# Twenty places instead of eighteen for the expert matrices of a hybrid decoder step

## What is computed

```python
def grouped_moe(h, w_router, b_router, w_gate, w_up, w_down):
    logits = (t @ w_router) + b_router
    probs = jax.nn.softmax(logits, axis=-1)
    # best group of 4 experts, then the best two experts in it -> comb[token, expert]
    act = jax.nn.silu(jnp.einsum('td,edf->tef', t, w_gate)) * jnp.einsum('td,edf->tef', t, w_up)
    act = act * comb[..., None]
    y = jnp.einsum('tef,efd->td', act, w_down)

def layer(x, c, past, ssm0, conv0, w, w_router, b_router):
    # adaLN; forgetting attention and Mamba-2 branch on h @ w_in; m = their gated sum
    x = x + gt1 * (m @ w['w_o'])
    h2 = rms_norm(x, w['g_norm2']) * (1 + sc2) + sh2
    x = x + gt2 * grouped_moe(h2, w_router, b_router, w['w_gate'], w['w_up'], w['w_down'])
```

## Time and profile before

| | |
|---|---|
| median of three runs | 815.74 us (815.09 to 819.5) |
| the profiled execution | 816.63 us, of it 815.0 us from the first to the last instruction |
| mean granted TensorE clock | 0.973 of full speed |
| TensorE busy | 764.1 us, 94% |
| bytes moved | 219.67 MB, 270 GB/s over the span |

### The profile page before, as it was taken

One profiled execution on the slowest core, in us unless ns is written; L12 is line 12 of the kernel. 1 busy time (PEld: TensorE's weight loads), 2 busy tenths in 40 slices (PEclk: granted clock), 3 DMA queues, 4 the chain that ended last, 5 costly groups with the idle time before them and its releaser, 6 DMA issues.

```text
span 815.0 us, 12510 instructions
## 1 busy us (share of the span) xinstructions
PE 764.1 (94%) x4573; PEld 531.0 (65%) x4573; DVE 366.3 (45%) x847; ACT 294.5 (36%) x731; POOL 95.4 (12%) x156
## 2 busy tenths in 40 slices
PE   3698999999998999999989999999599999999997
PEld 3475687778775777888878788888333444444434
DVE  2455457777772275687998201123211223121213
ACT  1213247656772135658873001013211222221213
POOL 3321011222101115221011000000000000000000
PEclk9999999999999999999999899999599999999999
DMA  9797465879866522369998984373679999999992
GB/s 289 239 355 225 148 179 165 293 238 317 273 228 207 157 62 68 101 182 396 335 293 293 333 314 132 114 281 136 256 301 418 421 420 422 420 420 421 421 418 93
DMA packets 93531, 219.67 MB, mean 270 GB/s; under 512 B 11792, under 2 KB 67672, under 8 KB 78980
## 3 DMA queue, kind: packets, MB, share of 16 engines
q1 hardware_dynamic: 78850, 181.71, 61.4%
q0 software_dynamic: 7984, 31.87, 11.9%
q10 hardware_dynamic: 6634, 5.25, 2.1%
HBM read 207.58 MB, written 13.22 MB: 271 GB/s over the span
## 4 chain that ended last, share of the span: by engine, by line
PE 63%; DMA 10%; SPq 9%; ACT 7%; DVE 5%; issue 3%; POOLq 1%; ACTq 1%; POOL 0%; DVEq 0%
PE bank L1639 14%; PE bank L1949 9%; PE bank L1870 7%; SPq L559 5%; PE bank L1971 5%; DMA out_ssm_sample<-arena 4%; PE bank L1572 4%; PE bank L1878 4%; PE bank L1635 4%; DMA arena<-in_w_down 3%; PE bank L1852 3%; PE bank L1990 2%; SPq L540 2%; PE bank L1593 1%; DVE conv_work L1305 1%
## 5 line engine op out<-in xcount | busy, mean ns | idle before, releaser
L1639 PE MATMUL bank<-h_normed,weight_ring 128*128 128x264 f32 x1024 | 238.9, 390 | 3.0 <-ACT conv_work L1005 3.0
L1639 PEld LDWEIGHTS bank<-h_normed,weight_ring 128*128 128x128 f32 x1024 | 192.9, 191 | 38.3 <-issue 3.5
L1949 PE MATMUL bank<-arena,h_normed 128*64 128x512 f32 x176 | 79.3, 606 | 0.0
L1870 PE MATMUL bank<-y_T,weight_ring 128*128 128x264 f32 x256 | 59.6, 397 | 0.0
L1949 PE MATMUL bank<-weight_ring,h_normed 128*64 128x512 f32 x192 | 56.3, 595 | 0.6 <-ACT h_normed L1047 0.6
L1870 PEld LDWEIGHTS bank<-y_T,weight_ring 128*128 128x128 f32 x256 | 50.1, 196 | 8.9
L1498 DVE TENSOR_TENSOR arena<-arena,bank 128x512 f32<-128x512 f32 x8 | 8.7, 1090 | 104.7 <-PE bank L1949 104.7
L1505 DVE SCALAR_TENSOR_TENSOR x_residual<-bank,modulation,x_residual 128x256 f32<-128x256 f32 x64 | 28.8, 484 | 57.9 <-PE bank L1990 57.9
L1572 PE MATMUL bank<-identity,arena 128*128 128x128 f32 (+5 forms) x236 | 32.0, 277 | 15.3 <-ACT arena L840 9.5
L1572 PEld LDWEIGHTS bank<-identity,arena 128*128 128x128 f32 (+5 forms) x236 | 26.8, 148 | 26.0 <-issue 11.7
L997 ACT ACTIVATE arena<-conv_out,expanded 128x128 f32<-128x128 f32 x128 | 38.3, 388 | 13.0 <-DVE arena L1381 11.1
(11 more groups left out here) (360 smaller groups left out, 1182.7 us busy)
## 6 DMA issues: line engine op xcount, KB each, us to landing
weight_ring<-in_w_in SPq DMA_DIRECT2D x36, 1024.0 KB, 5.8
weight_ring<-in_w_mod SPq DMA_DIRECT2D x22, 1024.0 KB, 9.8
arena<-in_w_up SPq DMA_DIRECT2D x14, 1024.0 KB, 20.0
weight_ring<-in_w_gate SPq DMA_DIRECT2D x14, 1024.0 KB, 20.1
arena<-in_w_down SPq DMA_DIRECT2D x11, 1024.0 KB, 26.8
weight_ring<-in_w_up SPq DMA_DIRECT2D x10, 1024.0 KB, 18.7
arena<-in_state_ssm POOLq DMA_DIRECT2D x8, 1024.0 KB, 8.7
out_ssm_sample<-arena POOLq DMA_DIRECT2D x8, 1024.0 KB, 9.4
```

The costliest lines, as they stand in the source:

```text
L1639: ins = mm(ps[:, 0:T], w, hT[:, c, :], start=c == 0, stop=c == KD - 1)
L1870: ins = mm(ps[:, 0:T], w, yT[:, c, :], start=c == 0, stop=c == NXB - 1)
L1949: ins = mm(banks[i][BLK * e:BLK * e + BLK, :], xg[:, 4 * h + c, BLK * e:BLK * e + BLK], ws[e][:, c, :], start=h == 0 and c == 0, stop=h == ...
```

## The change

Two places are added, so that NMS is 20.

- Place 16 is new: a tensor "early_small" of 128 x 2048 words takes the place of eight small tensors, which become slices of it. att_T and conv_work move to places 17 and 18.
- Place 19 is new and is in two parts of 4 KB a partition: the second half of the h2tok rows in conv_out (uf[:, D:D + 1024]) and 1024 words of a tensor "head_rows", in which head_work, dt_logf and cums now lie side by side. A piece in it is loaded by two DMAs of 512 KB, and its semaphore counts 48 instead of 32 a use, which it shares with place 18.
- SP issues m = 16 right behind m = 15, without waiting for ("hx", 2, 1); m = 17 behind that wait; m = 18 and m = 19 behind h2_st; freed(m - 20) starts with m = 20.
- TensorE takes its operands through rows_of, which finds the part; shapes, order and number of matmuls are as they were.

```diff
-        half += [attT[:].rearrange("p c t -> p (c t)")[:, 0:2048], work[:, 0:2048]]
-        NMS = len(half)
+        half += [early[:, 0:2048], attT[:].rearrange("p c t -> p (c t)")[:, 0:2048], work[:, 0:2048]]
+        quarter = (uf[:, D:D + 1024], heads[:, T:T + 1024])
+        NMS = len(half) + 1
+
+        def rows_of(s, kind, c):
+
+            w = (512, 512, 1024)[kind]
+            if s == NMS - 1:
+                return quarter[c * w // 1024][:, c * w % 1024:c * w % 1024 + w]
+            return half[s][:, c * w:c * w + w]
+
+        def landed_per_use(s):
+
+            return 48 if s // 2 == (NMS - 1) // 2 else 32
...
-                sp.dma_start(half[s], (wg, wu, wdn)[kind][2 * j + e][:, 2048 * h:2048 * h + 2048]).then_inc(moe_full[s // 2], 16)
+                src = (wg, wu, wdn)[kind][2 * j + e][:, 2048 * h:2048 * h + 2048]
+                if s == NMS - 1:
+                    for q in range(2):
+                        sp.dma_start(quarter[q], src[:, 1024 * q:1024 * q + 1024]).then_inc(moe_full[s // 2], 16)
+                else:
+                    sp.dma_start(half[s], src).then_inc(moe_full[s // 2], 16)
...
             load_expert(7)
+            load_half(16)
             filled_by(("hx", 2, 1))
-            load_half(16)
+            load_half(17)
             sp.wait_ge(h2_st, 48)
-            load_half(17)
+            load_half(18)
+            load_half(19)
             for m in range(NMS, 12 * NPAIR):
                 freed(m - NMS)
                 load_half(m)
...
-                        pe.wait_ge(moe_full[s // 2], (r * moe_uses(s) + use) * 32)
-                    ws.append(half[s].rearrange("p (k n) -> p k n", k=(4, 4, 2)[kind]))
+                        pe.wait_ge(moe_full[s // 2], (r * moe_uses(s) + use) * landed_per_use(s))
+                    ws.append([rows_of(s, kind, c) for c in range((4, 4, 2)[kind])])
```

More of the change, by code:

```diff
@@ L66, in build @@
         ident = sb("identity", [128, 128])
-        ntri = sb("neg_triangle", [128, 3 * 128 + 1])
-        triu = sb("upper_triangle", [128, 128])
+        early = sb("early_small", [128, 2048])
+        ntri, triu = early[:, 0:385], early[:, 385:513]
         onesf = sb("ones", [128, 128])
-        blk = sb("head_blocks", [128, 128])
+        blk = early[:, 513:641]
         striu = sb("strict_upper", [128, 128], BF16)
@@ L82, in build @@
         brow = sb("router_bias", [1, NE])
-        cT = sb("cond_T", [128, KD, 32])
-        wfd = sb("w_forget_dt", [128, KD, HB])
+        cT = early[:, 1025:1281].rearrange("p (k n) -> p k n", k=KD)
+        wfd = early[:, 641:1025].rearrange("p (k n) -> p k n", k=KD)
         wr = sb("w_router_sb", [128, KD, NE])
@@ L96, in build @@
         yT = yq[:, 0:NXB * T].rearrange("p (c t) -> p c t", c=NXB)
-        fd = sb("dt_logf", [HB, T])
-        acsT = sb("cums", [64 + HB, NP])
+        heads = sb("head_rows", [128, 4 * T + NP])
+        fd = heads[0:HB, 3 * T:4 * T]
+        acsT = heads[0:64 + HB, 4 * T:4 * T + NP]
         ex = sb("expand_in", [SH, 2 * NS + 1])
-        tokc = sb("token_cols", [128, 7 * 32])
+        tokc = early[:, 1537:1761]
         lft = sb("logf_tok", [128, 3, NH])
-        exo = sb("expanded", [128, NXB * (2 * NS + 1)])
+        exo = early[:, 1761:2033]
         dsk = exo[:, 0:NXB]
@@ L106, in build @@
         sm2 = sb("small", [128, 64])
-        fdw_all = sb("head_work", [128, 3, T])
+        fdw_all = heads[:, 0:3 * T].rearrange("p (a t) -> p a t", a=3)
         fdw = fdw_all[0:HB]
         tokrow = fdw_all[:, 0, :]
-        mrow = sb("mod_rows", [128, SW])
+        mrow = early[:, 1281:1537]
         stT = sb("conv_states", [128, NCB, 24])
@@ L461, in build @@
         o_fs = sem("ssm_prompt_stored")
-        moe_full = [sem(f"expert_half_pair_landed{i}") for i in range(9)]
+        moe_full = [sem(f"expert_half_pair_landed{i}") for i in range(10)]
         gate_half = sem("gate_first_half_used")
@@ L662, in _ @@
                                  pattern=[[-1, 128]], channel_multiplier=1), consts)
-            link(g.memset(cT[:], 0.0), consts)
+            link(g.memset(cT, 0.0), consts)
             link(g.memset(onesf[:], 1.0))
             link(g.memset(epsc[:], EPS))
-            link(g.memset(blk[:], 0.0))
+            link(g.memset(blk, 0.0))
             link(g.memset(blk[0:64, 0:64], 1.0))
@@ L669, in _ @@
             link(g.memset(qbd[:], 0.0), qbd_zero)
-            link(g.memset(ntri[:], -1.0))
-            link(g.affine_select(out=ntri[:], in_=ntri[:], compare_op=ALU.is_ge, fill=0.0, base=-128,
+            link(g.memset(ntri, -1.0))
+            link(g.affine_select(out=ntri, in_=ntri, compare_op=ALU.is_ge, fill=0.0, base=-128,
                                  pattern=[[1, 385]], channel_multiplier=-1))
-            link(g.affine_select(out=triu[:], in_=onesf[:], compare_op=ALU.is_ge, fill=0.0, base=0,
+            link(g.affine_select(out=triu, in_=onesf[:], compare_op=ALU.is_ge, fill=0.0, base=0,
                                  pattern=[[1, 128]], channel_multiplier=-1))
@@ L865, in _ @@
                 if k == "mod":
-                    release(act, fn(mrow[:], ps[:, 0:SW], ACT.Copy), j)
+                    release(act, fn(mrow, ps[:, 0:SW], ACT.Copy), j)
                 elif k == "ssq":
@@ L1337, in _ @@
                     release(dve, v.tensor_tensor(cbm, ps.rearrange("p (g k) -> p g k", g=SG),
-                                                 triu[:].unsqueeze(1).to_broadcast([128, SG, 128]), ALU.mult), j)
+                                                 triu.unsqueeze(1).to_broadcast([128, SG, 128]), ALU.mult), j)
                 elif k == "ab":
@@ L1641, in _ @@
                     pe.wait_ge(qk_sq, 1 if k == "kn" else 2 + j[1] // 4)
-                    ins = mm(ps[:, 0:T], blk[:], u[:, j[1] % 4, :], start=True, stop=True)
+                    ins = mm(ps[:, 0:T], blk, u[:, j[1] % 4, :], start=True, stop=True)
                 elif k == "kt":
@@ L1949, in gate_up @@
                                 ins = mm(banks[i][BLK * e:BLK * e + BLK, :], xg[:, 4 * h + c, BLK * e:BLK * e + BLK],
-                                         ws[e][:, c, :], start=h == 0 and c == 0, stop=h == 1 and c == 3,
+                                         ws[e][c], start=h == 0 and c == 0, stop=h == 1 and c == 3,
                                          tile_position=(0, BLK * e))
@@ L1971, in down @@
                                 ins = mm(banks[2 + q][BLK * e:BLK * e + BLK, :], aT[:, 2 * h + c, BLK * e:BLK * e + BLK],
-                                         ws[e][:, c, 512 * q:512 * q + 512], start=h == 0 and c == 0,
+                                         ws[e][c][:, 512 * q:512 * q + 512], start=h == 0 and c == 0,
                                          stop=h == 1 and c == 1, tile_position=(0, BLK * e))
```

## The result

| | before | after |
|---|---|---|
| median of 20 runs each | 816.89 us (814.43 to 824.24) | 820.6 us (815.77 to 824.99) |
| ratio | | 1.0037, 95% interval 1.002 to 1.0054 |
| profiled execution's span | 815.0 us | 818.9 us |
| mean granted TensorE clock | 0.973 | 0.972 |
| TensorE busy | 764.1 us | 766.4 us |

The kernel became slower by 3.0 us, with an interval of 1.6 to 4.4 us. That is under the 0.5% within which I had called it the same, but 820.6 us lies above my range of 812.9 to 818.9. The kernel before also came out at 816.89 us over 20 runs, where three had given 815.74.

A forecast was written before the change was run, and what follows sets the result against it. TensorE was taken to bound the expert stage. Waits -2.3, store +0.2 and first gather +2.9 summed to +0.8 us: 815.8 on the profiled span of 815.0, 816.5 on the median of 815.74; range 812.9 to 818.9.

The forecast's parts named there:

- What bounds the kernel: Expert stage: TensorE is the bound at 26.8 us a pair; transfers cost it 2.3 us at the very end.
- The rival in which the transfers bind: Expert stage: transfers are the bound, so two pieces less gain 5.0 us, to 810.8; chance 0.05.
- the two waits: TensorE's two waits for weights in the down matrices of pair 6 both go, a gain of 2.3 us.
- The slices and the divided place: Small tensors as slices cost zero; divided-place pieces take 2.64 us instead of 2.49, 0.45 us together, hidden by unused lead.
- the change doesn't do what it says: Late stream: something else sets the landings, the waits stay at 2.3 and the start costs 3.1: 818.8; chance 0.06.
- Piece 16 ahead of the stores: Before the experts: the early piece delays the last 32 KB store by 0.2 us, bounds 0 and 2.5.
- landed together with the end of everything, so the queues share: Last store: its landing with pieces 12 to 15 was read as sharing, the ground for taking 0.2 us.
- First in, first out: Last store: upper bound of 2.5 us if it waits behind every byte issued earlier.
- Pieces 17 to 19 beside the gather: First gather takes 7.7 us instead of 4.8, landing 2.9 us later at about 589.5, when all queued bytes are through.
- The clock: TensorE's slow matmuls at the experts' start shift with it; taken as zero, at most 1.7 us either way.
- The start that costs nothing: Store and gather don't feel the added pieces, only the waits go: 813.4, or 814.4 with 1 us on the gather; chance 0.27.
- transfers in line: Between hx's last row and the first expert matmul: bytes in issue order, store +2.5, gather +5.2, to 821.1; chance 0.12.

The follow-up runs named there:

- layout_only: The kernel before with only the small tensors laid out as slices, 18 places and the old load order: 818.62 us, ratio 1.0014.
- start_as_before: The changed kernel with 16 and 17 at their old points, 18 and 19 only after the gather landed: 815.99 us, ratio 0.9981 to the kernel before.
- after_fourth: The changed kernel run again unaltered: ratio 1.003 to the kernel before.
- after_fifth: The changed kernel run again unaltered, a second time in the same job: ratio 1.0006 to the kernel before.
- the two runs with two pieces behind: The changed kernel with 18 and 19 issued only after the first gather landed, run twice: 815.39 and 813.12 us, ratios 0.9974 and 0.993 to before.
- before_copy: The kernel before, unaltered, timed as if it were an experiment: 817.74 us, ratio 1.0006.
- four_behind_gather: The changed kernel with pieces 16 to 19 issued only after the first gather landed: 813.83 us, ratio 0.9954 to the kernel before.
- kept_busy: four_behind_gather plus six unread matmuls in TensorE's waits before the experts: 811.22 us, ratio 0.9925 to the kernel before.
- none_ahead: The changed kernel with 16 issued together with 17 behind the sample rows of hx, run twice: 818.38 and 818.62 us, ratios 1.0009 and 0.9996 to before.
- before_two_behind_gather: The kernel before, 18 places, with pieces 16 and 17 issued only after the first gather landed: 816.92 us, ratio 0.998.

## Why the prediction was off

**What bounds the kernel: right.** With 20 places TensorE waits for no weights and pairs stay at 26.82 us. The rival in which the transfers bind needed 5.0 us from the stream; it gave 2.6, where I had counted 2.3 for the two waits.

**The slices and the divided place: right.** layout_only shows no cost, and start_as_before, with the divided place in use, has its gain of 2.4 us in full. That the change doesn't do what it says is excluded.

**Piece 16 ahead of the stores: wrong.** I took 0.2 us between bounds of 0 and 2.5. In after_fourth and after_fifth, whose transposes were not slow throughout, the store takes 6.37 and 5.16 us, and 5.64 and 5.74 in the two runs with two pieces behind; the four profiles of the old order (before, before_copy, layout_only, start_as_before) have 4.52 to 4.88. That is 0.3 to 1.9 us, about 1. What the early piece costs beyond the store follows under the next heading.

Counted from A the landing goes 15.3 to 15.45 with neither piece 16 nor 17 issued by then (four_behind_gather, kept_busy), 16.9 to 17.65 in the order of before, 17.66 to 18.42 with 16 up front, and 19.25 to 19.37 in the three with slow transposes, which issued the store 1.4 to 2.4 us later. The cleanest pairs are the runs that issued it at A + 12.0: it landed at A + 16.9 in layout_only and both none_ahead, and at A + 17.66 to A + 18.42 in after_fourth and the two with two pieces behind, 0.8 to 1.5 us later. With nothing of 16 and 17 ahead it didn't follow its own issue: kept_busy issued it at A + 10.39, four_behind_gather at A + 12.02, and it landed at A + 15.31 and A + 15.45.

The argument that failed was "landed together with the end of everything, so the queues share": landing with the end of everything is what standing in line looks like, too, and no row told the two apart. The runs do: the store goes past piece 17, but not for nothing. By the Trainium skill's rule ("DMA: Bandwidth & Descriptors", Queues, rings and completion order) of turns between the queues the term was about 0; the trace agrees with it in that the store goes past piece 17, and not in the 0, since the store paid about 1 us. First in, first out, at 2.5 us, is excluded by the piece that the store went past. The measurement lies between the two.

**Pieces 17 to 19 beside the gather: right mechanism, mis-sized, and coupled to the step before.** The gather takes 7.46, 7.57, 7.87, 8.20 and 8.80 us in the five profiles, 7.98 on average, against 4.53 in the three of the old order: +3.4 where I had +2.9. I said that it can't be later than the last byte queued, at about 589 with A at 563.17, that is A + 25.8. none_ahead met this: A + 25.22 and A + 25.55. In the change the last byte comes later, though the bytes are the same, and that is the step that failed. I had treated the store's delay and the gather's as two terms, the second being bounded by a fixed end of the transfers. In none_ahead, pieces 18 and 19 are issued while the queue is still full, at A + 16.9. With 16 up front they are issued at A + 18.1 to A + 19.4, when the queue has nearly run dry (0.66 of the time at 584 to 586 in the profile after), and behind that hole the engines move 332 to 352 GB/s where none_ahead moved 402 to 430. From 584 to 592 the bytes of about 2.4 us of full transfer (at 425 GB/s) are missing in the profile after, against 0.2 in none_ahead from 584 to 588, and the last bytes come at A + 27.3 and not at A + 25.3. The gather itself lands another us behind the last bytes, at 593.24, where in none_ahead it landed with them. These two make up the 2.9 us.

Why the end moves is open. It isn't the size of the hole alone: in after_fifth the store landed at A + 18.06 and not at A + 19.37, piece 18 was issued 1.3 us earlier and the hole is about half as large (in the three us from A + 19 on, 0.7 us of full transfer is missing, against 1.6), and yet the gather lands at A + 28.30, since behind it the engines move less. Its windows (the columns of rows 1), in which A + 19 is 582.1:

```profile
582.00:584.00 2.00, 0.08 (x1) 0.00 (x0) 0.87 (x3) 0.00 (x0) 1.39 (x1) 0.50 0.90 279
584.00:586.00 2.00, 0.00 (x0) 0.00 (x0) 0.00 (x0) 0.00 (x0) 0.08 (x1) 0.50 0.96 389
586.00:588.00 2.00, 0.00 (x0) 0.00 (x0) 0.00 (x0) 0.00 (x0) 0.00 (x0) 0.50 0.96 272
588.00:590.00 2.00, 0.00 (x0) 0.00 (x0) 0.00 (x0) 0.00 (x0) 0.00 (x0) 0.50 0.86 340
```

So the late store and the hole go with piece 16 up front, and the later end does too; that the one causes the other isn't shown. Nor is the reason for the lower rate: rows of 4 KB as in the earlier trace rows would give 397, and none_ahead had them too.

Altogether the gather lands at A + 28.3 instead of A + 23.2 (the means), 5.1 us later, of which the runs give 2.2 to the two pieces more that are issued just before the gather (none_ahead against before) and 2.9 to piece 16 up front (after against none_ahead). My sum had 2.9 for the first and 0.2 for the second: it was the term of piece 16 that was mis-sized, and about 1 us of its 2.9 shows in the time of the store.

**The clock: about right.** I took zero, with 1.7 us either way. Turn 0 is 18.21 to 19.82 us in the five, 18.31 to 18.86 in the three of the old order: +0.4 on average, with a spread of 1.6 in the five.

**The rivals.** The start that costs nothing is refuted, and by none_ahead twice. The slower rival, transfers in line, at +5.4 us in all, had the place right, the start, with the store at about 1 of the 2.5 us and the gather at +3.4 of the 5.2. Its mechanism, bytes in the order of issue, is refuted by the store that goes past piece 17. With +2.9 us the result lies about in the middle between the forecast's +0.8 and the rival's +5.4. I had given it 0.12, a third of that beyond 819.8.

**The range.** Put on my base of 815.74, the measured +2.9 gives 818.6, just inside, though by a start that I had 2 us too small. The rest of the miss is the base: three runs said 815.74, twenty said 816.89, and in the four comparisons of the experiments the kernel before had medians of 817.48 to 818.29. The single profile's other 1.8 us, above A, are within what one kernel's executions scatter there (562.97 to 565.57 in the five of the change). The range had no term for that.

## What to carry to other kernels

- A small transfer on the critical path is priced by what is on the way when it is issued, and not by its size alone (the same gather took 3.4 to 8.8 us): here pieces of down (0), which TensorE first uses behind its second gate_up, delayed a store of 32 KB by 1 us and a gather of 0.27 MB by 3.4. Issue prefetches behind it: from A on, the kernel with twenty places is 2.9 us slower than the one before in one order and 5.1 us faster in another.
- When a load is released by the landing of something else, don't add delays as if each were alone: 0.2 and 2.9 us were forecast, and 5.1 came. Walk through the queue from the first issue on, look for the point at which it runs dry, and try the pair together.
- For a change of a few us, count from a marker just above it. From there five profiles of one kernel agreed within 1.6 us, and the start within 0.5, while the spans and even timed ratios scattered by as much as the effect.

## What the chip showed beside that

- The 0.27 MB gather takes 3.4 to 3.54 us from issue to landing when hardly anything is queued, 4.18 to 4.79 with one piece issued just before it, and with two issued just before it 6.9 to 7.24 where the queue had never run dry and 7.46 to 8.80 in the change.
- The 32 KB store on ScalarE's queue landed ahead of 1 MB pieces that SP's queue had been given before it: at 580.04, where they landed at 581.1 and 583.6 (none_ahead).
- Six matmuls that nobody reads, placed in TensorE's waits, brought the granted clock from 0.50 to 1.00 ahead of the experts and shortened the first gate_up from 15.31 to 13.95 us. Turn 0 became 1.35 us shorter and the stream behind it 1.24 us longer, with 1.3 us more of waits for weights.
- A stretch of sparse transposes ran at the lower or at the upper level of the clock in different executions of the same kernel (of five, three wholly at the lower, one mostly and one wholly at the upper). In this kernel it cost nothing, as the gather landed at the same place; in before_two_behind_gather, with none of the pieces from 16 on issued before the gather, the store and the gather came over 2 us later than in four_behind_gather.
